# Two blocks of the first expert's turned rows as products of X with the marks

## What is computed

```python
def expert_choice_moe(x, w_router, w_gate_up, w_down):
    cap = CAPACITY_FACTOR * S // N_EXPERTS            # 128
    aff = jax.nn.softmax((x @ w_router).astype(jnp.float32), axis=-1)
    gates, idx = lax.top_k(jnp.swapaxes(aff, 1, 2), cap)
    xs = x[bi, idx]
    g, u = jnp.split(jnp.einsum('becd,edf->becf', xs, w_gate_up), 2, axis=-1)
    out = jnp.einsum('becf,efd->becd', jax.nn.silu(g) * u, w_down) * gates[..., None]
    return jnp.zeros_like(x).at[bi, idx].add(out)
...
x = layer_norm(ALPHA * x + ffn, ln_ffn_g[layer], ln_ffn_b[layer])
```

## Time and profile before

| | us |
|---|---|
| median of 3 runs (4255.37 to 4257.45) | 4255.53 |
| the profiled execution, its own time | 4254.38 |
| its span in the profile | 4252.6 |
| TensorE busy (95% of the span) | 4046.5 |
| VectorE busy | 1541.9 |
| ScalarE busy | 1058.4 |
| GpSimd busy | 291.6 |

### The profile page before, as it was taken

One profiled execution on the slowest core, in us unless ns is written; L12 is line 12 of the kernel. 1 busy time (PEld: TensorE's weight loads), 2 busy tenths in 40 slices (PEclk: granted clock), 3 DMA queues, 4 the chain that ended last, 5 costly groups with the idle time before them and its releaser, 6 DMA issues. The chain is left out here.

```text
span 4252.6 us, 65884 instructions
## 1 busy us (share of the span) xinstructions
PE 4046.5 (95%) x28648; PEld 2283.4 (54%) x28648; DVE 1541.9 (36%) x3430; ACT 1058.4 (25%) x2104; POOL 291.6 (7%) x351
## 2 busy tenths in 40 slices
PE   7999999999999989998997999999899988999998
PEld 4555675596868674454554444444444444444443
DVE  2344333445453541214656411111455639111113
ACT  2233221333333320103552000001345331000003
POOL 0000000101110100000110000000000110000000
PEclk9999999999999999999998999999999998999999
DMA  3000101100000003212007999999411129999997
GB/s 99 26 26 7 51 17 41 30 4 26 3 26 5 20 10 133 73 20 50 1 1 283 304 317 320 315 321 305 143 35 40 55 76 330 301 314 322 312 325 247
DMA packets 315087, 566.97 MB, mean 133 GB/s; under 512 B 48000, under 2 KB 121888, under 8 KB 314800
## 3 DMA queue, kind: packets, MB, share of 16 engines
q1 hardware_dynamic: 299328, 505.61, 35.1%
q0 software_dynamic: 9504, 34.61, 3.4%
q10 hardware_dynamic: 5968, 22.55, 1.3%
HBM read 514.46 MB, written 48.23 MB: 132 GB/s over the span
## 5 line engine op out<-in xcount | busy, mean ns | idle before, releaser
L3247 PE MATMUL bank<-ring,m_picked_T 128*128 128x512 f32 x2048 | 899.8, 597 | 4.1 <-ACT m_picked_T L3330 4.1
L3247 PEld LDWEIGHTS bank<-ring,m_picked_T 128*128 128x128 f32 x2048 | 389.9, 192 | 483.0 <-issue 477.4
L3247 PE MATMUL bank<-ring,m_hidden_T 128*128 128x512 f32 x1024 | 455.1, 592 | 0.0
L3247 PEld LDWEIGHTS bank<-ring,m_hidden_T 128*128 128x128 f32 x1024 | 189.7, 190 | 215.3 <-issue 215.2
L3496 DVE TENSOR_TENSOR m_hidden<-m_hidden,bank 128x512 f32<-128x512 f32 x64 | 43.9, 686 | 507.5 <-ACT m_hidden L3336 507.5
L1446 PE MATMUL bank<-hnT,first_block 128*128 128x336 f32 (+3 forms) x544 | 181.3, 485 | 7.3 <-PEq L101 7.3
L3336 ACT ACTIVATE m_hidden<-bank 128x512 f32<-128x512 f32 x64 | 38.2, 597 | 540.4 <-PE bank L3247 540.4
L237 PE MATMUL bank<-xT,first_block 128*128 128x512 f32 x352 | 152.4, 593 | 2.8 <-ACT l_i L2964 1.7
L2553 PE MATMUL bank<-xT,a_weights 128*128 128x512 f32 x320 | 140.5, 592 | 0.8 <-ACT xT L2433 0.8
L1446 PEld LDWEIGHTS bank<-hnT,first_block 128*128 128x128 f32 x544 | 102.6, 194 | 67.2 <-issue 21.7
L3502 DVE COPY m_hidden_T<-bank 128x256 f32<-128x256 f32 x64 | 27.0, 422 | 276.0 <-PE bank L3240 276.0
(11 more groups left out here) (501 smaller groups left out, 6168.3 us busy)
## 6 DMA issues: line engine op xcount, KB each, us to landing
ring<-in_moe_w_gate_up SPq DMA_DIRECT2D x512, 512.0 KB, 7.5
ring<-in_moe_w_down SPq DMA_DIRECT2D x256, 512.0 KB, 4.6
first_block<-in_w_in SPq DMA_DIRECT2D x23, 512.0 KB, 3.8
w_block<-in_w_in SPq DMA_DIRECT2D x19, 512.0 KB, 3.8
x_rows<-X ACTq DMA_DIRECT2D x2, 4096.0 KB, 17.6
ring<-y_rows SPq DMA_DIRECT2D x16, 512.0 KB, 8.7
out_w<-in_w_out ACTq DMA_DIRECT2D x11, 512.0 KB, 11.6
first_block<-in_lru_w_in SPq DMA_DIRECT2D x11, 512.0 KB, 3.8
```

Of the source, the lines that this page charges most:

```text
L3247: m = pe.matmul(banks[j][:, :], lhsT[:, (i % 8) * P:(i % 8 + 1) * P], ring[:, i, j, :], start=i % 8 == 0, stop=i % 8 == KD - 1)
```

## The change

For expert 0 alone, TensorE makes the first two of the eight blocks of xs (PICKED = 2) without the gathered rows: behind the list it multiplies the transposed X, block d of each of the 8 tiles as weights, by the marks, and adds up over the tiles, into banks 6 and 7. That gives the chosen rows, already turned. ScalarE copies each block into xs. TensorE then multiplies slab 0, waits for `picked` and the gather, turns the six remaining blocks, multiplies slab 1 and goes on with slab 2. Since the picks read the marks of expert 0, VectorE waits for them before it writes those of expert 1. ScalarE copies 256 columns instead of 512 in the first of its two copies.

```diff
--- before.py
+++ after.py
@@ -3141,6 +3141,7 @@
         counted, first_counts = st.sem("counted"), sum((t > 0) + (t > 4) + 2 + t for t in range(NT))
         COUNTS = (first_counts, first_counts + 36)
         gathered, scattered = k.swaps[layer]
+        PICKED, first_picked, first_copied = 2, st.sem("first_picked"), st.sem("first_copied")
         x_turned, x_even, x_odd = (st.sem(n) for n in ("x_turned", "x_even", "x_odd"))
         used, sig, acted, h_turned, h_even, h_odd, y_even, y_odd = (st.sem(n) for n in (
             "used", "sigmoid", "acted", "h_turned", "h_even", "h_odd", "y_even", "y_odd"))
@@ -3225,11 +3226,15 @@
             for t in range(NT):
                 spread_tensor(pe, 1, t)
             list_tensor(pe, 0, ps[4])
-            pe.wait_ge(picked.sem, 2)
+            pe.wait_ge(row_in.sem, NT)
+            for d in range(PICKED):
+                for t in range(NT):
+                    m = pe.matmul(ps[6 + d][:, 0:P], X[:, t, d * P:d * P + P], chosen[:, t, :], start=t == 0, stop=t == NT - 1)
+                m.then_inc(*first_picked.up())
 
             def turn_tokens(e):
                 pe.wait_ge(gathered.sem, 16 * (e + 1))
-                for b in range(KD):
+                for b in range(0 if e else PICKED, KD):
                     m = pe.transpose(ps[4 + b // 4][:, (b % 4) * P:(b % 4) * P + P], xg[:, b * P:(b + 1) * P],
                                      c["ident"][:, :])
                 m.then_inc(*x_turned.up())
@@ -3253,11 +3258,17 @@
                 pe.transpose(ps[2][:, 0:NE], atf[:, :], c["ident"][0:NE, 0:NE])
                 pe.transpose(ps[2][:, NE:2 * NE], top[:, :], c["ident"][0:NE, 0:NE]).then_inc(*top_turned.up())
 
-            turn_tokens(0)
             for e in range(NE):
+                if e == 0:
+                    for d in range(PICKED):
+                        pe.wait_ge(first_copied.sem, d + 1)
+                        multiply(0, d, xs, ps[0:2])
+                        if d == 0:
+                            pe.wait_ge(picked.sem, 2)
+                            turn_tokens(0)
                 pe.wait_ge(x_even.sem, e + 1)
                 pe.wait_ge(x_odd.sem, e + 1)
-                for d in range(KD):
+                for d in range(0 if e else PICKED, KD):
                     multiply(e, d, xs, ps[0:2])
                 for d in range(KD):
                     if d == 5:
@@ -3326,8 +3337,9 @@
                     ac.dma_start(y_rows[t * P:(t + 1) * P, :], x).then_inc(*y_out[t % 2].up(16))
 
             def copy_tokens(e):
+                at = 0 if e else PICKED * P
                 ac.wait_ge(x_turned.sem, e + 1)
-                ac.activation(xs[:, 0:512], ps[4][:, :], ACT.Copy).then_inc(*x_even.up())
+                ac.activation(xs[:, at:512], ps[4][:, at:512], ACT.Copy).then_inc(*x_even.up())
                 if e == 0:
                     ac.activation(xs[:, 512:1024], ps[5][:, :], ACT.Copy).then_inc(*x_odd.up())
 
@@ -3355,6 +3367,9 @@
                 ac.wait_ge(*varied.now())
                 ac.activation(s[:, 2:3], s[:, 1:2], ACT.Exp, scale=-0.5).then_inc(*rooted.up())
 
+            for d in range(PICKED):
+                ac.wait_ge(first_picked.sem, d + 1)
+                ac.activation(xs[:, d * P:d * P + P], ps[6 + d][:, 0:P], ACT.Copy).then_inc(*first_copied.up())
             copy_tokens(0)
             scaled_rows()
             for e in range(NE - 1):
@@ -3431,6 +3446,7 @@
             for t in range(NT):
                 if x:
                     ve.wait_ge(listed[x - 1].sem, 1)
+                    ve.wait_ge(first_picked.sem, PICKED)
                 ve.tensor_scalar(chosen[:, t, :], places[:, :], rank[:, x, t:t + 1], None, ALU.is_equal).then_inc(*marked[x].up())
 
         def pick_vector(ve, x, bank):
```

## The result

The changed kernel takes 4266.85 us in the median of 12 runs (4262.29 to 4268.92), the kernel before 4256.07 us (4251.19 to 4259.38, 12 runs): 10.8 us more, a ratio of 1.0025 with a 95% interval of 1.0018 to 1.0033. The prediction was 4267.0 us, from an increase of 11.5 us laid on the median of three runs before, 4255.53.

A forecast was written before the change was run, and what follows sets the result against it. TensorE was taken as the bound, with hardly any room before ScalarE's sigmoid behind the y_rows writes. Going on later (2.8 + 4.3 us) plus restarts (4.4) made 11.5 us on 4255.53: 4267.0 us, range 4257.5 to 4273.

The forecast's parts named there:

- 32 pick records: TensorE behind expert 0's list: the 16 pick products, 21 records at half clock and 11 at full, take 5.7 us.
- TensorE early at turn_hidden(0, 0): TensorE reaches the turning of the first half of the hidden rows 5.4 and 4.1 us earlier, by layer.
- first write after the list, against before: ScalarE's first write to y_rows is issued 0.2 us later in the first layer, 0.6 in the second.
- first pair of writes: Distance between the first y_rows writes' pairs in scaled_rows, now beside slab loads: 7.05 us instead of 3.75.
- first to seventh write: ScalarE's y_rows writes ahead of the sigmoid: 22.8 us from first to seventh, where it was 18.36 and 18.66.
- TensorE goes on, against before: At turn_hidden(0, 0), after standing 8.2 and 8.4 us for act, TensorE continues 2.8 and 4.3 us later.
- restart at 1.2 GHz: After the idle stretch, turn_hidden and the slabs behind it run at the lower clock: 2.2 us lost per layer.
- rival 2: Pick records at double price, load and stream adding up: 9.4 us instead of 5.7, total 4274.4 us; chance 0.07.
- rival 1: The first y_rows writes don't get slower beside the loads: 3.0 us more in all, 4258.5 us; chance 0.15.
- rival 4: TensorE stalls at turn_hidden(0, 0) but its clock stays up: 7.1 us more, 4262.6 us; chance 0.08.
- Given back later: Behind the first experts, the loss stays: the other experts run at TensorE's pace, so none is recovered.
- Rival 3: Not slower: VectorE, not ScalarE, is the next limit; TensorE goes on 2.5 and 1.2 us earlier, 4251.8 us; chance 0.06.

The follow-up runs named there:

- e1: Changed kernel with scaled_rows cut up: four tiles ahead of the first sigmoid, four dealt out behind it; 4249.6 us, ratio 0.9988.
- e9: Changed kernel with scaled_rows dealt out, VectorE's rounds dealt anew and three blocks picked instead of two; 4246.8 us.
- e3: Changed kernel, but expert 1's first slab load is issued only when the first two y_rows writes have landed; 4260.5 us.
- e7: Kernel before plus the 16 picks, results unused: all eight blocks turned from the gathered rows, slab 0 behind them; 4262.6 us.
- e2: Changed kernel plus nine unused 128x512 products on TensorE ahead of turn_hidden(0, 0); 4260.4 us.

## Why the prediction was right

Its steps, each with what was measured, first and second layer:

| step | predicted | measured |
|---|---|---|
| 32 pick records | 5.7 | 6.31, 6.30 |
| TensorE early at turn_hidden(0, 0) | 5.4, 4.1 | 4.9, 3.6 |
| first write after the list, against before | +0.2, +0.6 | +0.8, +1.1 |
| first pair of writes | 7.05 | 6.81, 5.97 |
| first to seventh write | 22.8 | 21.82, 22.09 |
| TensorE goes on, against before | +2.8, +4.3 | +3.7, +3.6 |
| restart at 1.2 GHz | 2.2, 2.2 | 1.7, 2.3 |
| sum | 11.5 | 11.3 |

- **The bound.** Right. The prediction read from the earlier trace rows that the sigmoid stood 2.1 and 0.7 us short of holding TensorE up. e1 takes the sigmoid out from behind the last four writes and keeps all the work, and 15.4 us of the stretch come back.
- **The picks' price.** The clock stayed low longer than taken: at 0.11 us a record at full clock, 6.31 us are about 26 records at half clock where I took 21. Right was that load and stream lie side by side: 0.11 us in e9. In its list of what overlaps, the Trainium skill (TensorE: Matmul & The Clock Gate, Part 3) lets them overlap only for different groups of rows; this trace differs, and rival 2 falls.
- **The writes.** The direction is right, and e3 shows that the loads slow the first pair; at 6.81 and 5.97 us against 3.76 and 3.75, rival 1 falls. In the sizes four errors partly cancel. The first write came 0.5 us later than taken. The three pairs together were 1.0 and 0.7 us shorter. The 0.3 us from act to the first transpose, which no row shows, were 0.06 and 0.05. And in the first layer the eighth write fell 3.48 us behind the seventh instead of 1.99, which no term had; without that one TensorE would have gone on 1.5 us sooner there.
- **The number.** That 4267.0 stands so near 4266.85 is luck: by layer TensorE went on 0.9 us later and 0.7 us earlier than forecast, and the forecast increase of 11.5 us stands against 10.8 in the medians.
- **The cause was told too narrowly.** The prediction gave the early slab as what slows the writes. That holds for most of the first pair: without an early slab (e7) it took 4.84 and 3.75 us. But e7 still loses 9.2 of 11.3 us, 3.7 in going on later and 5.5 behind it at the lower clock. Being early there is no gain, and TensorE's full clock in the first group is enough to lose.
- **The restart.** Right: e2 shows it as 1.6 and 2.3 us, by keeping TensorE at work in the wait, and rival 4, by which the clock stays up, falls.
- **Given back later.** Nothing: the stretches from expert 1 to the list of the other experts are the same (37.0 us in both layers of both kernels; 22.48 of them for the first 52 records).
- **Rival 3,** the other side, needed the sigmoid out from behind the writes. Made so in e1, its 37.0 us came out as 36.65 in both layers.

The profiled execution of the changed kernel is 14.1 us longer than that of before, the medians 10.8. The first list starts 2.3 us later in it (2292.30 and 2290.03), ahead of all that the change touches. That, and the gather of expert 2, where TensorE stood 3.65 and 2.84 us before and 3.6 and 4.4 after, is not the change's, as far as these runs can tell: over all of them this wait lies between 0.8 and 4.7 us.

## What to carry to other kernels

Before filling a gap of the busiest engine, look at the next place where it waits for another, and at how much room that wait has: here it was 2.1 and 0.7 us, and a saving of 5 us ahead of it turned into a wait of 8. In a program written in order, long work that nobody needs soon (eight copies and writes) should not stand ahead of a short step that the busiest engine needs. An engine that uses its buffers earlier, or faster, also reloads them so, beside transfers that had the DMA engines to themselves.

## What the runs showed of the hardware

- Work added to TensorE made the stretch shorter: nine unused products in the wait saved 3.2 us up to expert 1 over both layers, since the clock then stayed at 2.4 GHz (e2).
- After an idle stretch of 2.57 us (e1) TensorE ran the transposes and the twelve records behind them at 2.4 GHz. After 4.43 us (e3) the four transposes still ran at 2.4 GHz (0.66 us), and the clock fell behind them; after 4.24 us (e7, second layer) they already ran at 1.2 GHz (1.12 us). So in these runs the length of the idle stretch alone did not tell where the clock fell. In the changed kernel's stretch the granted clock was still 1.00 in its first 2 us and 0.75 on average in the next 6.
- A 512 KB write landed in 2.7 us with no slab load beside it (e3). Beside the loads, in the changed kernel, the first two took 5.7 and 7.0 us in the first layer and 4.9 and 5.4 in the second.
